# Hybrid decoder trunk: nine of the eleven down-projection chunks of each FFN as seven block products

## The chip, the cores and the metric

The kernel runs on one core of one Trainium2 chip. The metric is the device time of one execution in microseconds (us): the median over the runs shown, beside one execution that the hardware profiler recorded.

## The reference, cut to what matters

Four layers, each a macaron pair: FFN, token mixer, FFN. There are 256 tokens, the model width is 1024 and the FFN width is 2816, all in float32. Eight of the twelve sublayers are this FFN, wrapped in two norms:

```python
def swiglu(x, wg, wu, wd):
    return (jax.nn.silu(x @ wg) * (x @ wu)) @ wd

x = x + 0.5 * rmsnorm(swiglu(rmsnorm(x, g[0]), ffn1_wg[i], ffn1_wu[i], ffn1_wd[i]), g[1])
xn = rmsnorm(x, g[2])          # then the token mixer (convolution, attention or mLSTM)
...
x = x + 0.5 * rmsnorm(swiglu(rmsnorm(x, g[4]), ffn2_wg[i], ffn2_wu[i], ffn2_wd[i]), g[5])
```

## The kernel before, in words

**Precision.** Each float32 operand is split into a high part rounded to the matmul type and a low part, the rest. A product is three matmuls into one accumulator: high by high, high by low, low by high (`products`, L504 to L508).

**Weights.** All weights come from DRAM as one stream of pieces of 128 x 2048 floats (1 MB). SyncE's queue loads piece p into one of `RAW` = 3 raw slots as soon as the split of piece p-3 is complete (`piece_split`). ScalarE makes the high part with `high(p)` (L1103) and VectorE the low part with `low(p)` (L1494), in one of `RING` = 6 slots, which TensorE frees with `piece_used`. The counts of these semaphores are positions in the stream, so the pieces are split in stream order.

**One FFN.** The hidden width of 2816 is worked on as 22 blocks of 128 columns (`BLOCKS`), two to a chunk (11 `CHUNKS`). `block(i)` makes gate and up of one block, 16 products of 256 columns into one PSUM bank, 0 or 1 by turns. ScalarE does `silu_of` (L1147) on the gate half, VectorE `times_up` (L1552) multiplies by the up half and gives h; `h_high` and `h_low` split h into `oT_hi` and `oT_lo`. `down_both(c)` then adds the chunk's part of the output for both tiles of 128 tokens and both halves of 512 columns into banks 4 to 7: eight products, seven of 512 columns and one in two parts of 256. The first four blocks (`early_block`) put the tokens on the partitions, so their h has to be turned over by TensorE (`transpose_h`, L632) before `oT_hi` and `oT_lo` are made.

**Order on TensorE in an FFN.** Early blocks 0 to 3, block 4, `down_both(0)`, block 5, `down_both(1)`, then a loop of units (`unit(c)`: blocks 2c+2 and 2c+3, then `down_both(c)`), then blocks 18 to 21 in a row, and the last stretch: for each tile and half the three chunks 8, 9 and 10. A tile's half is complete, and `y_ready` is signalled, after 18 of these matmuls. `transpose_next`, which turns over tile 0 of the next sublayer's normed input (L547), stands in front of chunk 10 of the last tile and half.

**Order on ScalarE and VectorE.** Both run a fixed list of instructions in order. At the end of an FFN both split two pieces of the next sublayer (`high`/`low` of `w0 + FFN_PIECES + 1` and `+ 2`) after the last split of h, and then come to `joint_part`: squares and their sums on ScalarE (`square_y`, L1112, and `square_x`, L1121), `gain_y` (L1502, L1506, L1509), `update_x` (L1519) and `pre_norm` (L1524, L1529) on VectorE, with small powers on GpSimd between them. They lead from `y_ready` to `xn`, which `transpose_next` reads.

Of the kernel before, what the change touches and what calls it, by code (L numbers as in the profile page):

```python
# [28 lines left out]
P = 128  # L29
D = 1024  # L30
# [10 lines left out]
EARLY = 4  # L41
WARM_UP = 17
# [69 lines left out]

def early_piece(c):

    return 2 * c


def block_piece(i):

    return {4: 4, 5: 6}.get(i, i + i // 2 - 1) if i < BLOCKS - 2 else 3 * CHUNKS - 5 + i - (BLOCKS - 2)  # L120


def down_piece(c):

    return {0: 5, CHUNKS - 3: 3 * CHUNKS - 3, CHUNKS - 2: 3 * CHUNKS - 2, CHUNKS - 1: 3 * CHUNKS - 1}.get(c, 3 * c + 4)


def build(nc, x_in, gains, first_gain, stream, gate_w, gate_b, conv_k, ident_in, rope_in, att_mask_in, ml_mask_in,
          tri_in, out):
    with ExitStack() as ctx:  # L130
# [52 lines left out]

        region = sb("region", [P, REGION])
        used = [0]
# [31 lines left out]
        h = from_region([2, SEQ])  # L217
# [33 lines left out]
        hT_split = sem("hT_split")  # L251
        oT_high_done = sem("oT_high_done")
# [132 lines left out]

        H_SPLITS = EARLY // 2 + BLOCKS - EARLY

        def splits_up_to(i):
            return EARLY // 2 + i - EARLY + 1

        def h_slot(i):

            return i % 4 if i < BLOCKS - 2 else 4 + i - (BLOCKS - 2)
# [105 lines left out]
        def _(pe):  # L499
# [4 lines left out]
            def products(acc, lh, ll, rh, rl, start, stop):  # L504

                nc.tensor.matmul(acc, lh, rh, start=start, stop=False)  # L506
                nc.tensor.matmul(acc, lh, rl, start=False, stop=False)  # L507
                return nc.tensor.matmul(acc, ll, rh, start=False, stop=stop)  # L508
# [50 lines left out]
            def ffn(sub):  # L559
                h0, s0, w0 = BLOCKS * ffn_no(sub), H_SPLITS * ffn_no(sub), w_of(sub)  # L560

                def bank_free(i):
                    if i >= 2:

                        pe.wait_ge(h_ready, h0 + i - 1)
# [24 lines left out]
                def block(i, p, turn=0, before=0):  # L590

                    bank_free(i + before)
                    weights_ready(p + RING * turn)
                    for e in range(2):
                        for k in range(KD):
                            cols = slice(k * 256 + e * P, k * 256 + (e + 1) * P)
                            last = products(ps[:, GU_BANK + i % 2, e * SEQ:(e + 1) * SEQ], w_high[:, p % RING, cols],
                                            w_low[:, p % RING, cols], xT_high()[:, k, :], xT_low()[:, k, :],
                                            k == 0, k == KD - 1)
# [37 lines left out]
                def down(c, p, t, turn=0):  # L637

                    weights_ready(p + RING * turn)
                    for half in range(2):  # L640
                        for j in range(FT):
                            cols = slice(j * D + half * 512, j * D + half * 512 + 512)
                            tok, at = slice(t * P, (t + 1) * P), h_slot(FT * c + j)
                            if t == 1 and half == 1 and j == FT - 1:

                                for part in range(2):
                                    some = slice(cols.start + part * 256, cols.start + part * 256 + 256)
                                    last = products(ps[:, Y_BANK + 2 * t + half, part * 256:part * 256 + 256],
                                                    oT_hi[:, at, tok], oT_lo[:, at, tok], w_high[:, p % RING, some],
                                                    w_low[:, p % RING, some], False, False)  # L650
                                continue
                            last = products(ps[:, Y_BANK + 2 * t + half, :], oT_hi[:, at, tok], oT_lo[:, at, tok],
                                            w_high[:, p % RING, cols], w_low[:, p % RING, cols],
                                            c == 0 and j == 0, False)
                    if t == 1:
                        last.then_inc(piece_used, 1)

                def down_both(c, turn=0):

                    if c < EARLY // 2:  # L660
                        pe.wait_ge(hT_split, s0 + c + 1)
                    else:
                        pe.wait_ge(hT_split, s0 + splits_up_to(FT * c + 1) + 4 * turn)
                    for t in range(TILES):
                        down(c, w0 + down_piece(c), t, turn)
# [21 lines left out]
                down_both(0)  # L687
                block(5, w0 + block_piece(5))
                down_both(1)
                with pe.Fori(0, (CHUNKS - 5) // 2) as turn:  # L690
                    unit(2, turn)
                    unit(3, turn)

                for i in range(BLOCKS - 4, BLOCKS):
                    block(i, w0 + block_piece(i))
                for t in range(TILES):
                    for half in range(2):
                        for c in range(CHUNKS - 3, CHUNKS):
                            p = w0 + down_piece(c)
                            if t == 0 and half == 0:  # L700
                                pe.wait_ge(hT_split, s0 + splits_up_to(FT * c + 1))
# [3 lines left out]
                            for j in range(FT):  # L705
# [4 lines left out]
                                                c == CHUNKS - 1 and j == FT - 1)  # L710
# [1350 lines left out]
```

## Time and profile before

| what | value |
|---|---|
| median of 3 runs | 2031.4 us (2030.3 to 2031.6) |
| span of the profiled execution | 2029.3 us |
| TensorE busy, share of the span | 2020.3 us, 100% |
| weight loads (PEld) | 1883.4 us, 93% |
| VectorE (DVE) | 1202.4 us, 59% |
| ScalarE (ACT) | 965.8 us, 48% |
| GpSimd (POOL) | 26.5 us, 1% |

The profiled execution has no time of its own beside its span; the span leaves out what lies before the first and after the last instruction. Matmuls overlap in the records, so their durations exceed the time that one adds: that time is the distance between the starts of two successive ones. A VectorE or ScalarE instruction that does not depend on the one before it also starts some 0.08 us before that one's record ends.

### The profile page before, as it was taken

The numbers are of one execution on the slowest core, as the hardware profiler recorded it, in microseconds if no ns is written. First come the engines' busy times: TensorE is split into PE (matmuls) and PEld (weight loads), VectorE is DVE, ScalarE is ACT, GpSimd is POOL, SyncE is SP. The second block draws the span as 40 slices with busy tenths as digits, with TensorE's granted clock in tenths as the row PEclk, the third lists the DMA queues.
The fourth block names the chain that finished last, engine by engine and source line by source line (L and its number), as shares of the span: only waits on it lengthen the run. The fifth ranks groups of instructions, "written<-read, shape, count | busy, mean of one in ns | idle before, by whom it ended". The sixth has DMA issues, their size and how long they took to land.

```text
span 2029.3 us, 36261 instructions
## 1 busy us (share of the span) xinstructions
PE 2020.3 (100%) x15078; PEld 1883.4 (93%) x15078; DVE 1202.4 (59%) x1335; ACT 965.8 (48%) x1176; POOL 26.5 (1%) x52
## 2 busy tenths in 40 slices
PE   9999999999999999999999999999999999999998
PEld 7999989998999999988998999998999999998998
DVE  6446675556545887766456555656456554676453
ACT  6444544444444665665444444645444444545442
POOL 0000000000000000000000000000000000000000
PEclk9999999999999999999999999999999999999999
DMA  8554646455554644436544655634544655555541
GB/s 319 203 193 158 249 153 242 186 187 208 187 191 161 224 171 164 150 126 249 187 186 172 223 187 188 226 138 177 204 186 166 228 189 196 192 196 194 205 186 63
DMA packets 56270, 386.08 MB, mean 190 GB/s; under 512 B 6752, under 2 KB 7136, under 8 KB 11232
## 3 DMA queue, kind: packets, MB, share of 16 engines
q1 hardware_dynamic: 52416, 372.07, 49.7%
q10 hardware_dynamic: 3744, 12.39, 1.9%
q8 instruction: 88, 1.44, 0.3%
q14 instruction: 22, 0.18, 0.0%
HBM read 383.39 MB, written 1.05 MB: 189 GB/s over the span
## 4 chain that ended last, share of the span: by engine, by line
PE 98%; DVE 1%; issue 0%; DMA 0%; ACT 0%; POOL 0%; DVEq 0%; POOLq 0%
PE ps L506 24%; PE ps L508 24%; PE ps L507 24%; PE ps L512 6%; PE ps L514 6%; PE ps L513 6%; PE ps L525 2%; PE ps L528 2%; PE ps L531 2%; PE ps L547 1%; PE ps L863 0%; PE ps L632 0%; PE ps L839 0%; DVE w_low L1494 0%; PE ps L874 0%
## 5 line engine op out<-in xcount | busy, mean ns | idle before, releaser
L1494 DVE TENSOR_TENSOR w_low<-raw,w_high 128x2048 fp32r<-128x2048 f32 x351 | 801.8, 2290 | 312.9 <-ACT w_high L1103 312.8
L1103 ACT ACTIVATE w_high<-raw 128x2048 fp32r<-128x2048 f32 x351 | 668.8, 1911 | 50.9 <-DMA raw<-stream 41.3
L506 PE MATMUL ps<-xT_both,w_high 128*128 128x256 f32 x2304 | 638.0, 277 | 0.0
L507 PE MATMUL ps<-xT_both,w_high 128*128 128x256 f32 x2304 | 637.0, 276 | 0.0
L508 PE MATMUL ps<-xT_both,w_low 128*128 128x256 f32 x2304 | 636.8, 276 | 0.0
L507 PEld LDWEIGHTS ps<-xT_both,w_high 128*128 128x128 f32 x2304 | 433.2, 188 | 0.0
L506 PEld LDWEIGHTS ps<-xT_both,w_high 128*128 128x128 f32 x2304 | 432.7, 188 | 0.0
L508 PEld LDWEIGHTS ps<-xT_both,w_low 128*128 128x128 f32 x2304 | 432.5, 188 | 0.0
L1147 ACT ACTIVATE region<-ps 128x256 f32<-128x256 f32 x176 | 67.4, 383 | 663.0 <-PE ps L508 641.8
L506 PE MATMUL ps<-w_high,oT_hi 128*128 128x512 f32 (+1 forms) x896 | 337.6, 377 | 0.0
L508 PE MATMUL ps<-w_high,oT_lo 128*128 128x512 f32 (+1 forms) x896 | 335.6, 375 | 0.0
L507 PE MATMUL ps<-w_low,oT_hi 128*128 128x512 f32 (+1 forms) x896 | 335.6, 375 | 0.0
L1552 DVE TENSOR_TENSOR region<-region,ps 128x256 f32<-128x256 f32 x176 | 74.0, 421 | 343.1 <-ACT region L1147 342.9
L512 PE MATMUL ps<-xT_both,w_high 128*128 128x256 f32 x736 | 207.3, 282 | 0.0
L514 PE MATMUL ps<-xT_both,w_high 128*128 128x256 f32 x736 | 204.7, 278 | 0.0
L513 PE MATMUL ps<-xT_both,w_low 128*128 128x256 f32 x736 | 204.7, 278 | 0.0
L508 PEld LDWEIGHTS ps<-w_high,oT_lo 128*128 128x128 f32 x896 | 168.4, 188 | 30.6
L506 PEld LDWEIGHTS ps<-w_high,oT_hi 128*128 128x128 f32 x896 | 168.5, 188 | 30.1 <-issue 0.3
L507 PEld LDWEIGHTS ps<-w_low,oT_hi 128*128 128x128 f32 x896 | 168.6, 188 | 29.3
L512 PEld LDWEIGHTS ps<-xT_both,w_high 128*128 128x128 f32 x736 | 138.7, 188 | 0.7
L513 PEld LDWEIGHTS ps<-xT_both,w_low 128*128 128x128 f32 x736 | 138.5, 188 | 0.0
L514 PEld LDWEIGHTS ps<-xT_both,w_high 128*128 128x128 f32 x736 | 138.3, 188 | 0.0
(180 smaller groups left out, 1827.3 us busy)
## 6 DMA issues: line engine op xcount, KB each, us to landing
raw<-stream SPq DMA_DIRECT2D x351, 1024.0 KB, 4.8
gain<-gains ACTq DMA_DIRECT2D x23, 512.0 KB, 5.0
x<-x_in SPq DMA_DIRECT2D x2, 512.0 KB, 4.5
raw<-stream SPq DMA_DIRECT2D x2, 512.0 KB, 6.3
region<-rope_in SPq DMA_DIRECT2D x1, 512.0 KB, 6.1
out<-x SPq DMA_DIRECT2D x1, 512.0 KB, 2.6
att_mask<-att_mask_in SPq DMA_DIRECT2D x1, 320.0 KB, 6.2
out<-x SPq DMA_DIRECT2D x1, 256.0 KB, 2.1
```

The source lines that it names most:

```text
L506: nc.tensor.matmul(acc, lh, rh, start=start, stop=False)
L507: nc.tensor.matmul(acc, lh, rl, start=False, stop=False)
L508: return nc.tensor.matmul(acc, ll, rh, start=False, stop=stop)
L512: nc.tensor.matmul(acc, lh, rh, start=start, stop=False)
L513: nc.tensor.matmul(acc, ll, rh, start=False, stop=False)
L514: return nc.tensor.matmul(acc, lh, rl, start=False, stop=stop)
L525: nc.tensor.matmul(acc, xT_high()[:, k, tok], w_high[:, slot, cols], start=k == 0, stop=False)
L528: nc.tensor.matmul(acc, xT_low()[:, k, tok], w_high[:, slot, cols], start=False, stop=False)
L1103: nc.scalar.activation(w_high[:, p % RING, :], raw[:, p % RAW, :], ACT.Copy).then_inc(piece_high, 1)
L1147: nc.scalar.activation(silu[:, i % 2, :], ps[:, GU_BANK + i % 2, 0:SEQ], ACT.Silu).then_inc(silu_done, 1)
L1494: nc.vector.tensor_tensor(w_low[:, p % RING, :], raw[:, p % RAW, :], w_high[:, p % RING, :], ALU.subtract).then_inc(piece_split, 1)
L1552: nc.vector.tensor_tensor(h[:, i % 2, :], silu[:, i % 2, :], ps[:, GU_BANK + i % 2, SEQ:2 * SEQ], ALU.mult).then_inc(h_ready, 1)
```

## The change

Nine of the eleven chunks (`SEVENS`) are added with Strassen's scheme in its seven-product form. A chunk's product is a 256 x 256 by 256 x 1024 matmul: two tiles of tokens by two blocks of hidden rows, and two blocks of hidden rows by two halves of 512 columns. Instead of eight products it makes seven, each from one sum of token blocks and one sum of weight blocks, each accumulated in a PSUM bank of its own (1 to 7) over the nine chunks. So:

- The gate and up blocks 4 to 19 all use bank 0, and each waits for `times_up` of the block before it.
- For each such chunk VectorE makes four sums of the weight blocks (`sum_w`, three instructions, written to `sums`, which is the memory of `xn`) and four sums of h (`sum_h`, three instructions). ScalarE and VectorE split three weight blocks as they are (`corners_high`, `corners_low`: 1536 columns) and the four sums (`sums_high`, `sums_low`: 2048 columns, in the place of the piece's `high` and `low`), and seven blocks of h at once (`seven_h_high`, `seven_h_low`: 896 columns).
- `unit(c)` on TensorE is block 2c+2, three of the seven products, block 2c+3, the other four. Unit 8 is added after the loop. VectorE and ScalarE are one or two pieces less ahead of TensorE in the stream than before.
- After chunk 8, ScalarE copies bank 1 out (`first_part_out`) and VectorE joins the seven sums into banks 4 to 7 (`join`, seven instructions of 512 columns). Blocks 20 and 21 run meanwhile. The last stretch has two chunks, 9 and 10, in place of three.

```diff
+SEVEN = ((1, 1, "corner", 0), (6, 3, "corner", 2), (7, 7, "corner", 1), (4, 2, "sum", 3), (5, 5, "sum", 0),
+         (2, 6, "sum", 2), (3, 4, "sum", 1))
+SEVEN_SPLIT = 3
+def gu_bank(i):
+    return GU_BANK + (i % 2 if i < EARLY or i >= BLOCKS - 2 else 0)
...
-                def bank_free(i):
-                    if i >= 2:
+                def bank_free(i, turn=0):
+                    if i == BLOCKS - 1:
+                        pe.wait_ge(first_copied, ffn_no(sub) + 1)
+                    elif EARLY < i <= BLOCKS - 2:
+                        pe.wait_ge(h_ready, h0 + i + 4 * turn)
+                    elif i >= 2:
...
+                def seven(c, first, last, turn=0):
+                    p = w0 + down_piece(c)
+                    if first == 0:
+                        pe.wait_ge(hT_split, s0 + c + 1 + 2 * turn)
+                        weights_ready(p + RING * turn)
+                    for bank, row, kind, col in SEVEN[first:last]:
...
+                        done = products(ps[:, bank, :], oT_hi_flat[:, tok], oT_lo_flat[:, tok], rh, rl, c == 0,
+                                        c == SEVENS - 1)
...
                 def unit(c, turn=0):
-                    block(2 * c + 2, w0 + block_piece(2 * c + 2), turn, 4 * turn)
-                    block(2 * c + 3, w0 + block_piece(2 * c + 3), turn, 4 * turn)
-                    down_both(c, turn)
+                    block(2 * c + 2, w0 + block_piece(2 * c + 2), turn)
+                    seven(c, 0, SEVEN_SPLIT, turn)
+                    block(2 * c + 3, w0 + block_piece(2 * c + 3), turn)
+                    seven(c, SEVEN_SPLIT, len(SEVEN), turn)
...
-                        for c in range(CHUNKS - 3, CHUNKS):
+                        for c in range(CHUNKS - 2, CHUNKS):
                             p = w0 + down_piece(c)
                             if t == 0 and half == 0:
+                                if c == SEVENS:
+                                    pe.wait_ge(joined, 7 * (ffn_no(sub) + 1))
```

VectorE's list for one FFN afterwards (ScalarE's goes with it: `silu_of`, `high`, `corners_high`, `sums_high`, `seven_h_high`):

```python
def unit(c, turn=0):
    p = w0 + block_piece(2 * c + 2)
    times_up(sub, 2 * c + 2, turn)
    low(p + 3, turn)
    low(p + 4, turn)
    sum_w(sub, c + 1, turn)
    times_up(sub, 2 * c + 3, turn)
    sum_h(sub, c + 1, turn)
    corners_low(sub, c + 1, turn)
    seven_h_low(sub, c + 1, turn)
    sums_low(sub, c + 1, turn)
# start: times_up(1) low(4) sum_w(0) corners_low(0) sums_low(0) times_up(2) low(6) times_up(3) sum_h(0) sum_w(1)
#        seven_h_low(0) times_up(4) corners_low(1) sums_low(1) sum_h(1) low(8) seven_h_low(1) low(9) times_up(5)
#        sum_h(2) sum_w(2) seven_h_low(2) corners_low(2) sums_low(2), then units 2 to 7
# end:   times_up(18) low(29) low(30) times_up(19) chunk_low(9) low(31) join times_up(20) low(32) h_low(20)
#        low(33) times_up(21) h_low(21) low(34) low(35)
```

ScalarE's unit: `silu_of(2c+2)`, `high(p+4)`, `corners_high(c+1)`, `silu_of(2c+3)`, `sums_high(c+1)`, `seven_h_high(c+1)`, `high(p+6)`. Its start has `copy_hT` (the turned h from PSUM to SBUF) after `silu_of(3)` and after `silu_of(4)`.

## Rows read from the trace of the kernel before

**Rows 1.** The page, busy time and share of each engine, and the core's clock.

```profile
PE 2020.3 (100%) x15078; PEld 1883.4 (93%) x15078; DVE 1202.4 (59%) x1335; ACT 965.8 (48%) x1176; POOL 26.5 (1%) x52
...
core 0: 2029.3 us, clock 0.999
```

**Rows 2.** Waits of TensorE: us in total, times, longest.

```profile
PE ps L502 <- DVE ones L1487: 1.1, 1, 1.1
```

**Rows 3.** Timeline of TensorE, one `down_both` in the loop: start us, us, instruction.

```profile
68.06 0.28 PE L508 MATMUL ps<-xT_both,w_low 128*128 128x256 f32 x1
68.18 0.39 PE L506 MATMUL ps<-w_high,oT_hi 128*128 128x512 f32 x1
...
72.95 0.28 PE L506 MATMUL ps<-w_high,oT_hi 128*128 128x256 f32 x1
...
73.67 0.29 PE L506 MATMUL ps<-xT_both,w_high 128*128 128x256 f32 x1
```

**Rows 4.** Groups by shape on VectorE: count, busy us, mean ns, idle before.

```profile
L1494 DVE TENSOR_TENSOR w_low<-raw,w_high 128x2048 fp32r<-128x2048 f32 x351 | 801.8, 2290 | 312.9 <-ACT w_high L1103 312.8
L1552 DVE TENSOR_TENSOR region<-region,ps 128x256 f32<-128x256 f32 x176 | 74.0, 421 | 343.1 <-ACT region L1147 342.9
...
L1584 DVE TENSOR_TENSOR region<-region 128x512 f32<-128x512 f32 x24 | 16.6, 692 | 0.8
...
L1558 DVE TENSOR_TENSOR oT_lo<-ps,oT_hi 128x512 fp32r<-128x512 f32 x16 | 11.0, 688 | 0.5
...
L1612 DVE TENSOR_TENSOR w_low<-raw,w_high 128x1024 fp32r<-128x1024 f32 x1 | 1.2, 1219 | 0.0
L1881 DVE CUSTOM_DVE_ANT_0 region<-ps,region 128x128 f32<-128x128 f32 x4 | 1.2, 292 | 16.2 <-PE ps L997 16.2
```

**Rows 5.** Groups by shape on ScalarE.

```profile
L1103 ACT ACTIVATE w_high<-raw 128x2048 fp32r<-128x2048 f32 x351 | 668.8, 1911 | 50.9 <-DMA raw<-stream 41.3 <-PE ps L508 6.3 <-PE ps L514 2.6
...
L1295 ACT ACTIVATE oT_hi<-region 128x512 fp32r<-128x512 f32 x8 | 5.1, 633 | 26.2 <-DVE region L1733 26.2
```

**Rows 6.** Timeline in the loop: `silu_of` after each of two blocks, then `times_up`.

```profile
62.94 0.38 ACT L1147 ACTIVATE region<-ps 128x256 f32<-128x256 f32 x1 [6.65 <-PE ps L508]
...
68.38 0.38 ACT L1147 ACTIVATE region<-ps 128x256 f32<-128x256 f32 x1 [2.95 <-PE ps L508]
...
68.88 0.42 DVE L1552 TENSOR_TENSOR region<-region,ps 128x256 f32<-128x256 f32 x1 [1.09 <-ACT region L1147]
```

**Rows 7.** Timeline of VectorE in the mLSTM: an instruction that waits for the one before.

```profile
1341.80 0.17 DVE L1886 TENSOR_SCALAR region<-region 128x2 f32<-128x2 f32 x1
1342.00 0.16 DVE L1888 TENSOR_TENSOR region<-region 128x2 f32<-128x2 f32 x1
```

**Rows 8.** DMA issues: count, KB each, us from issue to landing.

```profile
raw<-stream SPq DMA_DIRECT2D x351, 1024.0 KB, 4.8
```

**Rows 9.** Timeline at the start of the fourth sublayer, an FFN.

```profile
480.46 0.38 ACT L1147 ACTIVATE region<-ps 128x256 f32<-128x256 f32 x1 [1.42 <-PE ps L508]
...
482.68 4.49 DVE L1494 TENSOR_TENSOR w_low<-raw,w_high 128x2048 fp32r<-128x2048 f32 x2 [1.38 <-ACT w_high L1103]
...
491.71 0.38 PE L632 MATMUL ps<-ident,region 128*128 128x128 f32 x2
...
497.59 0.38 PE L632 MATMUL ps<-ident,region 128*128 128x128 f32 x2
```

**Rows 10.** Timeline at the end of the third sublayer, an FFN.

```profile
454.47 4.49 DVE L1494 TENSOR_TENSOR w_low<-raw,w_high 128x2048 fp32r<-128x2048 f32 x2 [1.38 <-ACT w_high L1103]
458.88 0.15 DVE L1502 TENSOR_SCALAR mean_first<-mean_y 128x1 f32<-128x1 f32 x1
...
459.52 0.60 ACT L1112 ACTIVATE xn<-ps 128x512 f32<-128x512 f32 x1 [2.71 <-PE ps L508]
...
460.24 0.16 DVE L1506 TENSOR_TENSOR mean_eps<-mean_y,mean_first 128x1 f32<-128x1 f32 x1 [0.61 <-ACT xn L1112]
...
464.45 1.28 DVE L1529 SCALAR_TENSOR_TENSOR xn<-x,rstd_x,gain 128x1024 f32<-128x1024 f32 x1 [0.66 <-POOL rstd_x L1954]
...
466.12 1.03 PE L547 MATMUL ps<-ident,xn 128*128 128x128 f32 x8
```

More of the change, by code:

```diff
@@ L588, in early_block, with block @@
                         last.then_inc(gu_ready, 1)
[L590 to L592 removed]
+                def block(i, p, turn=0):
+                    bank_free(i, turn)
                     weights_ready(p + RING * turn)
@@ L635, in transpose_h @@
                         last.then_inc(hT_in_psum, 1)
[L637 to L656, printed above, removed]
@@ L1650, in ffn @@
                 times_up(sub, 1)
                 low(w0 + 4)
-                low(w0 + 5)
+                sum_w(sub, 0)
+                corners_low(sub, 0)
+                sums_low(sub, 0)
                 times_up(sub, 2)
                 low(w0 + 6)
-                low(w0 + 7)
                 times_up(sub, 3)
-                early_h_low(sub, 0)
+                sum_h(sub, 0)
+                sum_w(sub, 1)
+                seven_h_low(sub, 0)
+                times_up(sub, 4)
+                corners_low(sub, 1)
@@ L1658, in ffn @@
+                sums_low(sub, 1)
+                sum_h(sub, 1)
                 low(w0 + 8)
-                times_up(sub, 4)
-                early_h_low(sub, 1)
+                seven_h_low(sub, 1)
                 low(w0 + 9)
-                h_low(sub, 4)
-                low(w0 + 10)
                 times_up(sub, 5)
-                low(w0 + 11)
-                h_low(sub, 5)
-                low(w0 + 12)
-                with dve.Fori(0, (CHUNKS - 5) // 2) as turn:
+                sum_h(sub, 2)
@@ L1669, in ffn @@
+                sum_w(sub, 2)
+                seven_h_low(sub, 2)
+                corners_low(sub, 2)
+                sums_low(sub, 2)
+                with dve.Fori(0, (SEVENS - 3) // 2) as turn:
                     unit(2, turn)
                     unit(3, turn)
-                for i in range(BLOCKS - 4, BLOCKS):
-                    times_up(sub, i)
-                    if i < BLOCKS - 1:
-                        low(w0 + block_piece(i) + 5)
-                    h_low(sub, i)
+                times_up(sub, BLOCKS - 4)
@@ L1676, in ffn @@
+                low(w0 + 29)
+                low(w0 + 30)
+                times_up(sub, BLOCKS - 3)
+                chunk_low(sub, SEVENS)
+                low(w0 + 31)
+                join(sub)
+                times_up(sub, BLOCKS - 2)
+                low(w0 + 32)
+                h_low(sub, BLOCKS - 2)
+                low(w0 + FFN_PIECES)
+                times_up(sub, BLOCKS - 1)
+                h_low(sub, BLOCKS - 1)
                 low(w0 + FFN_PIECES + 1)
```

251 lines of the change are left out of this document (181 added, 70 removed).

## The prediction

> **What bounds the kernel now.** I read the page first: TensorE is busy for the whole span at its full clock, while VectorE works 59% of it and ScalarE 48% [rows 1]. Then the waits of TensorE: after the start-up it waits for nobody that the list names [rows 2]. So the time is the sum of the matmuls' pitches. An edit gains by issuing fewer matmuls, and loses wherever TensorE has to wait. Both have to be counted, since nothing of today's time is a wait that could be won back. The timelines then give the pitches and the cover of each chain.
>
> **What is removed.** The first 21 matmuls of a `down_both`, seven products of 512 columns, take 72.95 - 68.18 = 4.77 us, 0.2272 us each; the whole, with its eighth product in two parts, takes 73.67 - 68.18 = 5.49 us [rows 3]. `seven` issues just such 21 matmuls, so a chunk saves 0.72 us. Chunk 8 stood in the last stretch without the split product (24 x 0.2272 = 5.45) and saves 0.68. That is 8 x 0.72 + 0.68 = 6.4 us an FFN, and **51 us** for eight.
>
> The Trainium skill ("TensorE: Matmul & The Clock Gate", Back-to-back issue gap) gives some 131 ns a matmul of 512 columns in a stream with weight loads. The trace disagrees with 227 ns [rows 3]; by the page the saving would be 72 x 3 x 0.131 = 28 us and everything below would end some 23 us higher. I go by the row.
>
> **What is added, in durations.** VectorE's two-input instructions fit 0.155 us + one column per 1.04 ns: 128 columns 0.29, 256 0.42, 512 0.69, 1024 1.22, 2048 2.29, with PSUM or without [rows 4]. Between them: 896 columns 1.09, 1536 columns 1.76. Two that don't depend on each other overlap by 0.08; a dependent one starts 0.03 after the end of the other (1341.80 + 0.17 to 1342.00) [rows 7]. So `sum_w` = 1.22 + 0.69 + 0.69 + two gaps = 2.66, `sum_h` = 0.29 + 0.42 + 0.29 + gaps = 1.06. ScalarE: 2048 in 1.91 and 512 in 0.63, so 0.832 ns a column [rows 5]: 1536 in 1.49, 896 in 0.95, 1024 in 1.06.
> VectorE per unit is then 0.42 + 2 x 2.21 + 2.66 + 0.42 + 1.06 + 1.68 + 1.01 + 2.21 less overlaps = 13.7 us. The unit on TensorE is two blocks of 68.38 - 62.94 = 5.44 [rows 6] and one `seven` of 4.77, 15.65 us. VectorE fits in, at 88%.
>
> **The loop.** Let P be the end of block 2c+2. `silu_of` starts at P + 0.21 and `times_up` at P + 0.7, ending at 1.13 [rows 6]. The next block needs it now (one bank), after three products of 2.04: 0.85 spare. VectorE does `low`, `low`, `sum_w` until 8.1. Its raw piece is asked for when `sums_low(c)` ends, at P - 1.1, and lands 4.8 later [rows 8], at 3.8; VectorE wants it at 5.5. Block 2c+3 ends at 7.48, `times_up` runs 8.2 to 8.6, `sum_h` to 9.6, `corners_low` to 11.3, `seven_h_low` to 12.3 (ScalarE's `sums_high` and `seven_h_high` are through by 11.0) and `sums_low`, for which the next `seven` waits, ends at 14.6. TensorE comes to it at 15.65. So the loop costs **nothing**, with 1.0 us to spare. Bounds: nothing, and, if the new shapes take 10% more (1.4 us), 0.4 a unit, 48 units, 19 us.
>
> **The start of each FFN.** Times of the fourth sublayer. `silu_of(1)` at 480.46, `low(4)` starts at 482.68 [rows 9] and ends at 484.97. Then `sum_w(0)` to 487.6, `sums_high(0)` on ScalarE to 489.5 (VectorE's `corners_low` lies beside it), `sums_low(0)` to 491.8, `times_up(2)` to 492.2. But TensorE comes to the turning of that h at 491.71 [rows 9]: it waits 0.5. Block 4 (to the next turning 5.9 [rows 9]) ends at 498.15. Meanwhile VectorE does `low(6)`, `times_up(3)` to 494.7, `sum_h(0)` to 495.8, `sum_w(1)` to 498.4 and only then `seven_h_low(0)` to 499.5: `seven(0)` waits 1.35. The list then runs on without a hole: `sums_low(1)` 505.1, `sum_h(1)`, `low(8)`, `seven_h_low(1)` 509.4, `low(9)`, `times_up(5)` 511.9, `sum_h(2)`, `sum_w(2)`, `seven_h_low(2)`, `corners_low(2)`, `sums_low(2)` 520.6; TensorE comes to `seven(2)` at 519.95 and waits 0.65. Together 2.5 us a start, **20 us** for eight. Before, none of this waited. Bounds: 1.3 to 3.7, a `sum_w` less or half one more on each chain.
>
> **The end of each FFN, first wait.** Zero is now the end of block 18; 19 ends at 7.48, `seven(8)` at 10.2, block 20 at 15.65, block 21 at 21.1. VectorE: `times_up(19)` to 8.6, `chunk_low(9)` 9.75 to 11.0 (after ScalarE's 1.06), `low(31)` 11.6 to 13.8, behind `high(31)`; `join`, seven of 0.69 that overlap by 0.08, to 18.1; `times_up(20)`, `low(32)`, `h_low(20)`, `low(33)` to 23.2, `times_up(21)` to 23.5, `h_high(21)`, `h_low(21)` to H = 24.45. TensorE takes block 21, then chunk 9's six matmuls (1.36), and wants that h at 22.45. It waits 2.05. Before, there were two chunks of cover and no `join` in front. Bounds 1.5 to 3 by how a `join` instruction that writes PSUM is priced (0.61 to 0.75); no row has one on VectorE.
>
> **The end, second wait.** This is the large one. After H, `low(34)` and `low(35)` come first, as before: H was 454.47 - 1.38 = 453.09, and they ended at 458.96, H + 5.87 [rows 10]. From `mean_eps` of tile 0 to the end of its `xn` is 464.45 + 1.28 - 460.24 = 5.49 [rows 10]. Before, `mean_eps` waited for the second half of tile 0, squared from 459.52 [rows 10], and `xn` was ready 0.4 before TensorE came to the turning at 466.12. Between that half and the turning lay 18 + 12 matmuls, 6.8 us. With two chunks it is 12 + 6, 4.1 us. That half is now ready at H + 4.15, VectorE frees itself from the two splits at H + 5.8, does the first `gain_y`, `mean_eps` at H + 6.5, `xn` at H + 12.0. TensorE has 36 matmuls from H on (0.06 + 8.18) and comes at H + 8.24: it waits 3.75. All of this stands before the turning and nothing gives it back, since the next sublayer starts behind it. Seven FFNs have a next sublayer: 7 x (2.05 + 3.75) = 41; the last one has no pieces 33 to 35 to split, and waits 0.4. **41 us.** Bound below: were the two splits not in the way, `mean_eps` would come at H + 5.1 and the wait be 2.4.
>
> **The sum.** -51 + 0 + 20 + 41 = +10 us on the profiled 2029.3, which lies 2 us under the median of 2031.4: **2041 us**. Own range, from the bounds: 2031 to 2052.
>
> **The rivals.**
> (a) The other side: the turning isn't late, because tile 0's norm is ready when TensorE comes. Then the ends cost 14 us and not 41, and the time is 2015. For it speaks that today this chain never holds TensorE up [rows 2]; against it, that it is 5.49 + 0.8 us long and its cover falls from 6.8 to 4.1. It decides once the waits of an FFN together are under 6.4 us rather than 7.8: 1.4 less is enough for break-even, just what the two splits add. 0.15.
> (b) The waits are a little shorter everywhere (1.2 us an FFN): no change, 2031. 0.12.
> (c) VectorE becomes the bound of the loop. It needs 2.0 us more per unit in all, or 1.0 in the half behind `times_up(2c+3)`. For it: 88% load and three engines in a ring. Against: shapes near these are steady in the rows. At 10% more, 2060. 0.10.
> (d) The clock. It was granted in full, 0.999 of it [rows 1], while TensorE never stood still. Waits of some 4 us next to another of 2 are new. If after each long wait the next early block (5.5 us) ran at the lower level of 1.2 GHz and so took twice as long, that is 7 x 5.5 = 38 us, 2079; half of it is as likely, 2060. No row here shows a matmul at the lower level. The Trainium skill ("TensorE: Matmul & The Clock Gate", Part 1) says an idle stretch that is long enough lets the clock fall to half until the engine has been busy again; no row can bear it out. 0.06.
> My forecast holds 0.57.
>
> **How the numbers follow.** 0.2% is 4 us, about what a measurement of this kernel can tell from no change. Of my forecast's share 0.5 lies above 2035.5 and the rest within the band. Slower: 0.50 + 0.10 + 0.06 = 0.66. Same: 0.07 + 0.12 = 0.19. Faster: 0.15. The range 2020 to 2060 leaves out most of (a) and the upper part of (c) and (d).
>
> **What would show it.** TensorE's waits should be some 60 us: behind `times_up(2)` 0.5, `seven_h_low(0)` 1.35, `sums_low(2)` 0.65, `h_low(21)` 2.05 and `xn` 3.75 per FFN, none in the loop. VectorE's busy time should rise by 72 x 5.6 + 56 x 0.69 = 440 to about 1640 us (80%). If the wait in front of the turning is under 2.4, the last part is wrong; if waits stand in the loop, (c) is right; if the clock's row falls below 0.98, (d).

## The result: slower, and by more than predicted

| kernel | median us | range, runs | ratio to before, 95% |
|---|---|---|---|
| before | 2031.5 | 2030.3 to 2031.7, 4 | |
| after | 2069.9 | 2068.2 to 2070.9, 4 | 1.019 [1.0177, 1.0203] |

The change costs 38 us (1.9%). The forecast was 2041 with a range to 2060: the direction is right, the size is not.

**The page and the core's clock** of the changed kernel, which answer to [rows 1]:

```profile
PE 2018.0 (98%) x14670; PEld 1871.8 (90%) x14670; DVE 1617.4 (78%) x1831; ACT 1105.6 (53%) x1208; POOL 26.6 (1%) x52
...
core 0: 2069.0 us, clock 0.991
```

The 408 matmuls that went are the intended ones (216 of 512 columns, three for each of 72 chunks, and 192 by not halving a product). Yet TensorE's busy time fell by only 2.3 us, and the clock is no longer full. VectorE rose to 78%, near the 80% expected.

**The waits of TensorE** in the changed kernel (us in total, times, longest), where [rows 2] had one row:

```profile
PE ps L592 <- DVE xn L1619: 24.4, 7, 3.5
PE ps L551 <- DVE oT_lo L1662: 6.9, 8, 1.0
PE ps L551 <- DVE oT_lo L1715: 6.4, 8, 0.8
PE ps L683 <- DVE region L1642: 4.3, 9, 1.5
```

They are the turning, `seven_h_low(0)`, `h_low(21)` and `times_up(2)`: all four foreseen at these places, 42 us together where 60 were expected, and none in the loop. So 51 us saved and 42 us of waits would have made 2022. About 47 us came from elsewhere, and none of them is in this list.

**Where the time of one FFN went.** The fourth sublayer, cut at the same instructions of TensorE's timeline in three kernels (us; the third is the last experiment below):

| stretch | before | after | difference | predicted | eight chunks, split |
|---|---|---|---|---|---|
| turning of tile 0 to block 4 | 25.73 | 28.88 | +3.15 | +0.5 | 26.28 |
| block 4 to the first product of chunk 0 | 5.88 | 6.92 | +1.04 | +1.35 | 6.92 |
| chunk 0, block 5, chunk 1 | 16.55 | 15.31 | -1.24 | -1.44 | 15.34 |
| blocks 6 to 17 with chunks 2 to 7 | 98.32 | 96.40 | -1.92 | -3.67 | 94.91 |
| block 18 to the next turning | 36.76 | 41.67 | +4.91 | +5.12 | 37.58 |
| sum | 183.24 | 189.18 | +5.94 | +1.86 | 181.03 |

Two stretches show something new: the first, and the loop, where no wait stands. The last one agrees with the forecast in part by luck: blocks 18 to 21 take 0.8 us more than before (22.61 and 21.78), and the waits behind them are shorter by about as much.

**The loop.** TensorE's timeline of the changed kernel, start and duration, at both ends of two blocks of 48 matmuls:

```profile
362.14 0.39 PE L553 MATMUL ps<-corner,oT_lo 128*128 128x512 f32 x1
362.37 0.28 PE L551 MATMUL ps<-xT_both,w_high 128*128 128x256 f32 x1
362.49 0.28 PE L552 MATMUL ps<-xT_both,w_high 128*128 128x256 f32 x1
...
368.02 0.39 PE L551 MATMUL ps<-w_high,oT_hi 128*128 128x512 f32 x1
...
370.51 0.39 PE L553 MATMUL ps<-w_high,oT_lo 128*128 128x512 f32 x1
370.74 0.28 PE L551 MATMUL ps<-xT_both,w_high 128*128 128x256 f32 x1
...
376.39 0.39 PE L551 MATMUL ps<-corner,oT_hi 128*128 128x512 f32 x1
```

A block takes 368.02 - 362.37 = 5.65 us, and so does the next; [rows 6] gave 5.44, and the timeline of before has 5.44 to 5.46. That is 0.1177 us a matmul in place of 0.1134, at an unchanged record duration of 0.28: only the distance between starts shows it. The products of 512 columns run at (370.74 - 368.02) / 12 = 0.2267, as forecast. Before a block there now stands a product of 512 columns; before the change it was the halved product, 256 columns wide [rows 3].

**The end, and the clock.** The same timeline at the turning. The last field is the idle time before it and what ended it:

```profile
472.81 0.39 PE L553 MATMUL ps<-w_high,oT_lo 128*128 128x512 f32 x1
476.68 1.11 PE L592 MATMUL ps<-ident,xn 128*128 128x128 f32 x4 [3.48 <-DVE xn L1619]
...
478.30 0.78 PE L551 MATMUL ps<-w_high,oT_hi 128*128 128x512 f32 x1
478.87 0.63 PE L552 MATMUL ps<-w_low,oT_hi 128*128 128x512 f32 x1
479.30 0.63 PE L553 MATMUL ps<-w_high,oT_lo 128*128 128x512 f32 x1
```

And the windows over it: length, busy time of PE, PEld, DVE, ACT and POOL, granted clock, DMA share, GB/s:

```profile
470.00:475.00 5.00, 3.20 (x15) 2.30 (x13) 3.33 (x7) 1.66 (x4) 0.79 (x2) 1.00 0.93 388
475.00:480.00 5.00, 3.32 (x12) 3.03 (x13) 3.32 (x5) 1.26 (x3) 0.30 (x1) 0.53 0.02 7
480.00:485.00 5.00, 5.00 (x19) 3.98 (x19) 2.91 (x5) 3.32 (x4) 0.55 (x1) 0.79 0.00 0
485.00:490.00 5.00, 5.00 (x23) 4.11 (x22) 3.03 (x4) 0.72 (x3) 0.55 (x1) 1.00 0.44 159
```

After the wait of 3.5 us TensorE runs at its lower level of 1.2 GHz: matmuls of 512 columns stand 0.43 apart, not 0.227. The granted clock is 0.53, then 0.79, then full. Matmuls at the lower level follow all seven turnings behind an FFN, for a shorter or a longer time; in the kernel before they follow none. Rival (d) took place, and here it costs 5.77 - 3.17 = 2.6 us (from the turning to the fifth matmul of the next block, 482.45, against the same distance before). From tile 0's turning to tile 1's the seven places take 1.4 to 2.9 us longer than before, 15.0 us together.

**The chain of VectorE** that makes the turning late, its timeline in the changed kernel, which answers to [rows 10]:

```profile
464.26 0.43 DVE L1715 TENSOR_TENSOR oT_lo<-region,oT_hi 128x256 fp32r<-128x256 f32 x1 [0.48 <-ACT oT_hi L1240]
466.06 4.49 DVE L1584 TENSOR_TENSOR w_low<-raw,w_high 128x2048 fp32r<-128x2048 f32 x2 [1.38 <-ACT w_high L1148]
...
471.13 0.15 DVE L1596 TENSOR_TENSOR mean_eps<-mean_y,mean_first 128x1 f32<-128x1 f32 x1
...
475.34 1.28 DVE L1619 SCALAR_TENSOR_TENSOR xn<-x,rstd_x,gain 128x1024 f32<-128x1024 f32 x1 [0.66 <-POOL rstd_x L2122]
```

`h_low(21)` ends at H = 464.69, the two splits at H + 5.86 (predicted 5.8), `mean_eps` starts at H + 6.4 (6.5) and `xn` ends at H + 11.9 (12.0). The chain was read right to 0.1 us.

**New shapes of VectorE**, its groups by shape: count, busy us and mean ns, idle time before:

```profile
L1682 DVE TENSOR_TENSOR corner<-raw,corner 128x1536 fp32r<-128x1536 f32 x72 | 126.1, 1752 | 0.0
L1671 DVE TENSOR_TENSOR xn<-raw 128x1024 f32<-128x1024 f32 x72 | 87.9, 1220 | 0.0
L1662 DVE TENSOR_TENSOR oT_lo<-region,oT_hi 128x896 fp32r<-128x896 f32 x72 | 78.1, 1085 | 0.0
```

Predicted: 1.76, 1.22 and 1.09 us.

### The profile page after: what moved, and what is told of

Same layout as the page of the kernel before. It is cut to its first block, busy times and chain, and to the rows that moved or that the text cites. A ratio compares the mean times of both kernels' runs of the same rounds, so it can differ in the third digit from the quotient of the medians.

```text
span 2069.0 us, 36195 instructions
## 1 busy us (share of the span) xinstructions
PE 2018.0 (98%) x14670; PEld 1871.8 (90%) x14670; DVE 1617.4 (78%) x1831; ACT 1105.6 (53%) x1208; POOL 26.6 (1%) x52
## 4 chain that ended last, share of the span: by engine, by line
PE 81%; DVE 13%; ACT 3%; issue 1%; DMA 0%; POOL 0%; DVEq 0%; POOLq 0%; ACTq 0%
PE ps L551 19%; PE ps L553 19%; PE ps L552 19%; PE ps L557 6%; PE ps L559 6%; PE ps L558 6%; DVE w_low L1584 6%; ACT w_high L1148 2%; PE ps L592 1%; PE ps L570 1%; PE ps L573 1%; PE ps L576 1%; DVE w_low L1689 1%; DVE xn L1671 1%; ACT w_high L1223 1%
## 5 line engine op out<-in xcount | busy, mean ns | idle before, releaser
L1584 DVE TENSOR_TENSOR w_low<-raw,w_high 128x2048 fp32r<-128x2048 f32 x279 | 632.3, 2288 | 113.2 <-ACT w_high L1148 113.2
L551 PE MATMUL ps<-xT_both,w_high 128*128 128x256 f32 x2304 | 647.9, 281 | 0.0
L553 PE MATMUL ps<-xT_both,w_low 128*128 128x256 f32 x2304 | 647.2, 281 | 0.0
L552 PE MATMUL ps<-xT_both,w_high 128*128 128x256 f32 x2304 | 647.2, 281 | 0.0
L1148 ACT ACTIVATE w_high<-raw 128x2048 fp32r<-128x2048 f32 x279 | 531.9, 1911 | 28.5 <-DMA raw<-stream 17.3
L551 PE MATMUL ps<-w_high,oT_hi 128*128 128x512 f32 x544 | 217.7, 400 | 6.4 <-DVE oT_lo L1715 6.4
L552 PE MATMUL ps<-w_low,oT_hi 128*128 128x512 f32 x544 | 214.9, 395 | 0.0
L553 PE MATMUL ps<-w_high,oT_lo 128*128 128x512 f32 x544 | 214.8, 395 | 0.0
L557 PE MATMUL ps<-xT_both,w_high 128*128 128x256 f32 x736 | 207.7, 282 | 0.0
L558 PE MATMUL ps<-xT_both,w_low 128*128 128x256 f32 x736 | 205.2, 279 | 0.0
L559 PE MATMUL ps<-xT_both,w_high 128*128 128x256 f32 x736 | 205.2, 279 | 0.0
L1223 ACT ACTIVATE w_high<-xn 128x2048 fp32r<-128x2048 f32 x72 | 138.0, 1917 | 54.0 <-DVE xn L1676 54.0
L1689 DVE TENSOR_TENSOR w_low<-xn,w_high 128x2048 fp32r<-128x2048 f32 x72 | 164.7, 2287 | 2.5 <-ACT w_high L1223 2.5
L1216 ACT ACTIVATE corner<-raw 128x1536 fp32r<-128x1536 f32 x72 | 107.2, 1489 | 73.2 <-DMA raw<-stream 73.1
```

Of the source, the lines that this page charges most:

```text
L551: nc.tensor.matmul(acc, lh, rh, start=start, stop=False, skip_group_check=goes_on)
L552: nc.tensor.matmul(acc, lh, rl, start=False, stop=False, skip_group_check=goes_on)
L553: return nc.tensor.matmul(acc, ll, rh, start=False, stop=stop, skip_group_check=goes_on)
L558: nc.tensor.matmul(acc, ll, rh, start=False, stop=False)
L559: return nc.tensor.matmul(acc, lh, rl, start=False, stop=stop)
L1148: nc.scalar.activation(w_high[:, p % RING, :], raw[:, p % RAW, :], ACT.Copy).then_inc(piece_high, 1)
```

## The experiments

What was to be told apart: how much the blocks' pitch costs and what sets it; what the clock costs; and whether the waits at the two ends of an FFN can be had back by reordering, or only by more cover.

| kernel | median us | ratio to before, 95% | span, clock |
|---|---|---|---|
| `b_nosplit` | 2056.5 | 1.0124 [1.0107, 1.0141] | 2054.5, 0.999 |
| `a_split` | 2053.7 | 1.0111 [1.0094, 1.0128] | 2051.8, 0.993 |
| `a_splitfirst` | 2074.7 | 1.0198 [1.0179, 1.0217] | 2074.0, 0.992 |
| `a_warm` | 2056.6 | 1.0124 [1.0107, 1.0141] | 2053.1, 0.999 |
| `a_lows` | 2062.7 | 1.0152 [1.0135, 1.0169] | 2061.8, 0.995 |
| `a_low33` | 2071.3 | 1.0197 [1.0182, 1.0213] | 2069.4, 0.992 |
| `a_start` | 2082.4 | 1.0252 [1.0237, 1.0268] | 2079.7, 0.995 |
| `a_all` | 2062.7 | 1.0152 [1.0138, 1.0166] | 2060.9, 0.999 |
| `a_best1` | 2041.6 | 1.0049 [1.0035, 1.0062] | 2038.5, 1.000 |
| `a_best2` | 2042.3 | 1.0051 [1.0037, 1.0064] | 2040.8, 0.999 |
| `eight_plain` | 2026.0 | 0.9972 [0.9962, 0.9983] | 2024.1, 1.000 |
| `eight_split` | 2013.6 | 0.9914 [0.99, 0.9927] | 2011.8, 1.000 |

### The pitch alone: the kernel before without its halved product (`b_nosplit`)

```diff
-                            if t == 1 and half == 1 and j == FT - 1:
+                            if False:
```

> The kernel before (2031 us), with the split product as one of 512 columns and nothing else changed. Theory 1: the first block behind each down_both (and the blocks that follow without a break, if the pitch holds on) goes from 0.1134 to 0.1177 us a matmul: 9 to 17 blocks x 0.2 us x 8 = 15 to 28 us slower, less 8 x 8 x 0.05 = 3 for the split's own cost, 2043 to 2056 us. Rival: 2028 us, as only the split's own cost goes.

Measured: 25 us slower, with three matmuls fewer a chunk, the clock in full and no new wait of any size. Its timeline shows 96 matmuls, two blocks:

```profile
520.64 0.39 PE L508 MATMUL ps<-w_high,oT_lo 128*128 128x512 f32 x1
520.86 0.28 PE L506 MATMUL ps<-xT_both,w_high 128*128 128x256 f32 x1
...
532.17 0.39 PE L506 MATMUL ps<-w_high,oT_hi 128*128 128x512 f32 x1
```

(532.17 - 520.86) / 96 = 0.1178. The sum closes: 17 blocks x 48 x 0.0043 x 8 = 28 us, less some 3 us since 24 matmuls of 0.2267 take 5.44 and not 5.49. So the halved product of the kernel before is worth 25 us, and the change drops it.

### The halved product put back (`a_split`), at the other end of the group (`a_splitfirst`)

```diff
+                        if 0 < c < SEVENS - 1 and bank == SEVEN[last - 1][0]:
+                            for part in range(2):
+                                some = slice(part * 256, part * 256 + 256)
+                                done = products(ps[:, bank, some], oT_hi_flat[:, tok], oT_lo_flat[:, tok], rh[:, some],
+                                                rl[:, some], False, c == SEVENS - 1)
+                            continue
```

`a_splitfirst` has `SEVEN[first][0]` in the condition: the product behind the block is halved, not the one ahead of it. Chunks 0 and 8 are left as they are in both.

> The changed kernel (2070 us), with the last product before each block in two parts of 256 columns, as in the kernel before, for chunks 1 to 7. Chunk 8 keeps whole products and is the control inside the run. Theory 1, a block of 256-column matmuls runs at 0.1177 us a matmul when matmuls of 512 columns stand right before it, and at 0.1134 when some of 256 do: blocks 6 to 18 go to 0.1134, block 20 stays at 0.1177; 14 blocks x 0.2 us x 8 FFNs = 22 us less for TensorE, of which the waits at the FFNs' ends take back some 5, so 2050 to 2056 us. Rival, the slower pitch comes from the one bank, the memory layout or the busier VectorE and ScalarE: nothing changes, 2070 us.

> As a_split (2054 us), but the product in two parts is the first one of each part of a seven and not the last, so matmuls of 512 columns stand right before each block again. If the slow pitch comes from the neighbour right before the block, blocks run at 0.1177 us a matmul and the time is 2070 us. If it comes from how many matmuls stand between two blocks, or from a 256-column matmul anywhere between them, blocks stay at 0.1137 and the time is 2054 us.

Measured: `a_split` gains 16 us over the changed kernel, `a_splitfirst` nothing (its interval overlaps the changed kernel's) with the very same number of matmuls. Inside `a_split` one timeline holds both cases, block 18 behind the halved product of chunk 7 and block 19 behind a whole one of chunk 8:

```profile
430.09 0.28 PE L553 MATMUL ps<-w_high,oT_lo 128*128 128x256 f32 x1
430.21 0.29 PE L551 MATMUL ps<-xT_both,w_high 128*128 128x256 f32 x1
...
435.67 0.39 PE L551 MATMUL ps<-corner,oT_hi 128*128 128x512 f32 x1
...
437.50 0.39 PE L553 MATMUL ps<-corner,oT_lo 128*128 128x512 f32 x1
437.72 0.28 PE L551 MATMUL ps<-xT_both,w_high 128*128 128x256 f32 x1
...
443.38 0.39 PE L551 MATMUL ps<-w_high,oT_hi 128*128 128x512 f32 x1
```

5.46 us against 5.66. It is the width of what stands right ahead of the block that counts here. Over the whole trace of `a_split` there is no exception among the blocks from 5 on: most of those behind 256 columns run at 0.1134 to 0.1138 (the first of them in an FFN up to 0.1148), all behind 512 columns at 0.1177 to 0.1179. (`a_start` below has exceptions.) A halved product itself costs 0.03 to 0.05 us more. Thirteen blocks of an FFN are fast in this kernel (6 to 18), not the 14 that were expected: 13 x 0.2 x 8 = 21 us, less 13 halved products, 3 to 5 us, leaves the 16 us measured.

### The clock alone (`a_warm`)

Fifteen matmuls of 512 columns, whose results nobody reads, stand before the turning, in the time in which TensorE waited:

```diff
                             if t == 1 and half == 1 and c == CHUNKS - 1:
+                                for _ in range(15 if sub + 1 < SUBLAYERS else 0):
+                                    nc.tensor.matmul(ps[:, 0, :], oT_hi[:, 0, 0:P], w_high[:, p % RING, 0:512],
+                                                     start=True, stop=True)
                                 transpose_next(sub)
```

> The changed kernel, with 15 matmuls of 512 columns (3.4 us) into bank 0, whose result nobody reads, in the wait of 3.5 us in front of the turning of the next sublayer's input, seven times. Theory 2, that wait lets TensorE's clock fall to the lower level for the 5 us behind it and costs 2.7 us each time: the granted clock stays at 1.00, 2070 - 19 = 2051 us. Rival, the clock falls for another reason or the fall is hidden by other waits: 2066 to 2070 us.

Measured: 13.3 us faster than the changed kernel by the medians, 15.9 by the profiled spans, though it does more. The turning comes no earlier: from block 18 to it the fourth sublayer still takes 41.67 us. The gain is all behind it. The windows of this kernel over the turning show the full clock:

```profile
470.00:475.00 5.00, 4.91 (x27) 3.89 (x26) 2.69 (x5) 2.56 (x6) 0.55 (x1) 1.00 0.32 128
475.00:480.00 5.00, 5.00 (x24) 4.09 (x23) 4.23 (x6) 3.65 (x5) 0.55 (x1) 1.00 0.00 0
```

So the fall of the clock is worth 13 to 16 us, some 2 us a turning; the 15.0 us that the changed kernel loses between tile 0's turning and tile 1's are gone here (each of the seven is within 0.2 us of the kernel before). The Trainium skill ("TensorE: Matmul & The Clock Gate", Part 1) says that an idle stretch that is long enough halves the clock until the engine has been busy again. The traces agree, with 0.53 granted behind 3.5 us of waiting and 1.00 once the wait was filled.

### The end by reordering (`a_lows`, `a_low33`)

`a_lows` takes `low(34)` and `low(35)` out of the way, behind the first tile's `xn` and its `xT`. `a_low33` moves `low(33)` behind `h_low(21)`:

```diff
                 h_low(sub, BLOCKS - 1)
-                low(w0 + FFN_PIECES + 1)
-                low(w0 + FFN_PIECES + 2)
```

```diff
-                low(w0 + FFN_PIECES)
                 times_up(sub, BLOCKS - 1)
                 h_low(sub, BLOCKS - 1)
+                low(w0 + FFN_PIECES)
```

> The changed kernel, with VectorE's splits of the next sublayer's pieces 1 and 2 moved from the end of the FFN to behind xn of tile 0 and behind xT of tile 0. Theory 3, those two splits put xn of tile 0 off by 1.4 us: the wait in front of the turning falls from 3.5 to 2.1 us, and the clock doesn't fall any more if that is short enough: 2070 - 10 = 2060 us, and 2041 us with the clock. Rival, the next sublayer's first blocks then wait for the moved splits instead: 2066 us or more, with waits of TensorE for w_low.

> The changed kernel (2070 us), with the split of piece 33 (the next sublayer's first) behind h_low(21) in VectorE's list and not in front of times_up(21). VectorE now stands idle 0.5 and 1.4 us around h_low(21), behind ScalarE. If its list is what sets xn of tile 0, piece 33's split fills the second of these holes: the wait for h_low(21), 0.8 us, goes, and xn comes 1.4 us earlier, so 7 x 1.4 = 10 us less and a little more by the clock, 2057 to 2060 us. Rival, the list isn't what binds there: only the waits trade places, 2068 us.

Measured: `a_lows` is 7 us faster than the changed kernel, `a_low33` is not (+1.4). Waits of TensorE, first `a_lows`:

```profile
PE ps L592 <- DVE xn L1619: 19.6, 11, 2.2
```

then `a_low33`:

```profile
PE ps L592 <- DVE xn L1619: 29.3, 7, 4.2
PE ps L551 <- DVE oT_lo L1715: 3.8, 8, 0.5
```

In `a_lows` the first turning waits 2.23 us in place of 3.48, near the 2.4 that the prediction gave for this case; but four turnings of tile 1 now wait as well, and after a wait of 2.23 the clock still falls at most places: matmuls 0.42 to 0.43 us apart follow five of the seven turnings, for shorter times (0.995 granted over the whole kernel, 0.991 in the changed one). In `a_low33` what `h_low(21)` gains (6.4 to 3.8) the turning loses (24.4 to 29.3). VectorE has no room for the splits: ahead of the turning they put off tile 0's norm, behind it tile 1's.

### The start by reordering (`a_start`)

```diff
-                sum_w(sub, 1)
                 seven_h_low(sub, 0)
+                sum_w(sub, 1)
```

> The changed kernel, with seven_h_low(0) ahead of sum_w(1) in VectorE's list. If the wait of TensorE in front of the first seven comes from that place in the list, it falls from 0.85 us to nothing in each FFN, 8 x 0.85 = 7 us, 2063 us. Rival, VectorE's list has no hole there and all that follows comes later by the 1 us that seven_h_low then waits for ScalarE: the wait moves to the second or third seven, 2068 to 2072 us.

Measured: 12.5 us slower. Rows that have grown or are new among TensorE's waits, of `a_start`:

```profile
PE ps L551 <- DVE oT_lo L1662: 13.1, 9, 1.6
...
PE ps L551 <- ACT region L1197: 5.0, 8, 0.9
PE ps L551 <- DVE w_low L1689: 3.1, 8, 0.4
```

ScalarE's list was left as it was: `sums_high(1)` waits for the later `sum_w(1)`, and `silu_of(4)` and `copy_hT(1)`, which TensorE needs, are queued behind it. In the fourth sublayer the wait in front of the first seven is gone as intended, and 0.67 us inside it and 1.6 us in front of the second have come. Moving an instruction on one engine moves all that stands behind its consumer on another.

This trace also shows that the rule of the pitch is not complete. Block 5 stands behind a product of 512 columns here too, and in the fourth sublayer it runs at (523.16 - 517.82) / 47 = 0.1136:

```profile
517.01 0.50 PE L551 MATMUL ps<-w_high,oT_hi 128*128 128x512 f32 x1 [0.67 <-ACT region L1197]
...
517.82 0.28 PE L551 MATMUL ps<-xT_both,w_high 128*128 128x256 f32 x1
...
523.16 0.28 PE L553 MATMUL ps<-xT_both,w_low 128*128 128x256 f32 x1
```

Five of the eight blocks 5 and two of the blocks 7 of `a_start`, and one block 5 of `a_all`, are fast like this. TensorE had waited inside the products ahead of each of them, but it had ahead of slow blocks of this kernel too. From the last matmul of 512 columns to the block's first it is 0.233 to 0.236 us ahead of the fast ones and 0.226 to 0.229 ahead of the slow ones. So a product of 512 columns ahead is not enough by itself for the slow pitch, and what sets it is not known.

### All of it at once (`a_all`, `a_best1`, `a_best2`)

`a_all` joins `a_split`, `a_start`, `a_lows`, the later `low(33)`, a turning one product later and 6 unread matmuls ahead of it. `a_best1` leaves out `a_start` and `a_lows` and takes the halved product, the later `low(33)`, the later turning, and 8 unread matmuls; of these the later `low(33)` had not helped by itself, and the later turning was not measured by itself. `a_best2` adds to it a new order at the start on both engines:

```diff
-                sum_w(sub, 1)
+                corners_low(sub, 1)
                 seven_h_low(sub, 0)
                 times_up(sub, 4)
-                corners_low(sub, 1)
-                sums_low(sub, 1)
+                sum_w(sub, 1)
                 sum_h(sub, 1)
-                low(w0 + 8)
+                sums_low(sub, 1)
                 seven_h_low(sub, 1)
+                low(w0 + 8)
```

(on ScalarE `sums_high(1)` goes behind `copy_hT(1)`, `high(8)` behind `seven_h_high(1)`).

> All mendings together in the changed kernel: split products before blocks, seven_h_low(0) early, the splits of pieces 33 to 35 behind the last h and the norm of tile 0, the turning one product later in the last stretch, six matmuls that keep TensorE busy in what is left of the wait. From 2070: pitch -16, start -5, clock -13, ends 7 x (1.4 + 0.8 + 0.6) = -20, of which some 5 return as waits in the faster stream: about 2021 us, under the kernel before by 0.5%. Rival, the moved splits make the next sublayer wait, as a_lows showed in part: 2035 us.

> a_low33, with the split products of a_split, the turning one product later in the last stretch, and eight matmuls that keep TensorE busy in what is left of the wait. If the causes add up: 2070 - 16 (pitch) - 13 (clock) - 10 (piece 33) - 5 (turning) = 2026 us, or 2030 us with 4 us of waits that come back in the faster stream; level with the kernel before or just under. If they overlap, 2040 us.

> a_best1, with the lists at the FFN's start reordered on both engines: VectorE does corners_low(1) in the time in which ScalarE makes seven_h_high(0), and sum_w(1) after times_up(4); ScalarE does silu_of(4) and copy_hT(1) before it waits for sum_w(1), which held them up in a_start. If what a_start lost was the two instructions queued behind that wait, this gives 0.5 to 1 us an FFN, 4 to 8 us below a_best1. Rival, the whole start is bound by VectorE's work between times_up(1) and sums_low(2), and the order moves the wait to the third seven: the same as a_best1.

Measured: 2062.7, 2041.6 and 2042.3. `a_all` was expected at 2021, or 2035 by the rival, and missed both; it shows that the edits don't add up: its waits spread over seven rows of 3.8 us or more, of which `a_start` brings 4.6 and 4.3 and the later `xT` 7.1. `a_best1` comes out near the 2040 given for overlapping causes and is, with `a_best2`, the best form with nine chunks, still 10 us slower than before. What is left of waits in it:

```profile
PE ps L592 <- DVE xn L1628: 12.1, 7, 1.8
PE ps L551 <- DVE oT_lo L1671: 8.0, 8, 1.7
PE ps L551 <- DVE oT_lo L1724: 3.8, 8, 0.5
```

To 12.1 come the 56 unread matmuls, 56 x 0.227 = 12.7, together as much as the 24.4 of the changed kernel: TensorE stands without useful work in front of the turning for as long as ever, only warm. In `a_best2` the start's 8.0 become 1.2, and a new 7.0 appears behind `w_low` L1698 (`sums_low`), for the third group of products. That is the rival's outcome: the wait moves along with the order, and its sum stays (8.0 and 8.2), so VectorE's work binds the start in both orders.

### More cover: eight chunks (`eight_split`, `eight_plain`)

No list tried shortened the end by more than 7 us, so the cover is given back: `SEVENS` = 8, and chunk 8 is added in the last stretch as in the kernel before. `join` then lies beside blocks 18 to 21, which use banks 0 and 1 by turns:

```diff
-SEVENS = 9
+SEVENS = 8
...
-    return GU_BANK + (i % 2 if i < EARLY or i >= BLOCKS - 2 else 0)
+    return GU_BANK + (i % 2 if i < EARLY or i >= BLOCKS - 4 else 0)
...
-                        for c in range(CHUNKS - 2, CHUNKS):
+                        for c in range(CHUNKS - 3, CHUNKS):
```

and VectorE's end becomes:

```python
unit(SEVENS - 2)
times_up(sub, 16)
low(w0 + 26)
low(w0 + 27)
times_up(sub, 17)
chunk_low(sub, 8)
low(w0 + 28)
join(sub)
times_up(sub, 18)
...
times_up(sub, 19)
chunk_low(sub, 9)
...
times_up(sub, 20)
...
h_low(sub, 20)
...
times_up(sub, 21)
h_low(sub, 21)
```

> Only eight chunks (0 to 7) are made as seven products; chunks 8, 9 and 10 form the last stretch as in the kernel before, blocks 18 to 21 run in a row in banks 0 and 1 by turns, and the product that stands right before each block (chunks 1 to 6) is made in two parts of 256 columns. The computation is complete. If the end's waits came from the short last stretch, and the blocks' pitch from the 512-column product in front of them, both are gone: 8 FFNs save 8 x 0.72 = 5.8 us each (46), the starts still cost about 1.4 us each (11), and the row of blocks 18 to 21, behind a seven that isn't split, is slow (4 x 0.2 x 8 = 6): 1998 to 2006 us, clock 0.999, no wait behind xn. The rival: the end's chain is bound by VectorE's own backlog (the join and the four splits), whatever TensorE has as cover: then waits behind xn stay near 24 us and the clock falls, 2025 to 2035.

> The same with eight chunks, but no product is made in two parts. If the pitch of the blocks hangs on the product before them, all 96-matmul groups behind a 512-column product run at 0.1178 and the kernel is 14 to 20 us slower than its split form, 2014 to 2024 us. If the pitch was a matter of the waits and the clock at the end of an FFN, which are gone here, the two kernels agree within 4 us.

Measured: both beat the kernel before, `eight_split` by 18 us (0.9%), `eight_plain` by 5.5 us (0.3%). The clock of `eight_split` and its waits of TensorE:

```profile
core 0: 2011.8 us, clock 1.000
```

```profile
PE ps L555 <- DVE oT_lo L1680: 7.7, 8, 1.6
PE ps L687 <- DVE region L1660: 2.8, 8, 0.4
...
PE ps L596 <- DVE xn L1635: 0.3, 1, 0.3
```

The turning and `h_low(21)` have gone from the list, and the clock is full: the rival (VectorE's backlog binds whatever the cover) has fallen. (These two kernels also have `join` two blocks earlier in VectorE's list; no run parts this from the longer last stretch.) The two forms differ by 12.4 us where 14 to 20 were expected: the pitch returns in kernels with no wait at the end and no fall of the clock, so it is a cost of its own. I had `eight_split` too low by 8 us, and the table by stretches says where: blocks 5 and 17 run behind whole products of chunks 0 and 7 and are slow too (six slow blocks, 6 x 0.2 x 8 = 10, not four, 6); the eleven halved products of an FFN cost some 0.04 each, 4 us together; and the first unit, which waits a little for VectorE, takes 15.93 and not 15.77. Halving the products of chunks 0 and 7 that stand ahead of a block as well would be the next thing to try. It was not tried.

## Why the prediction was wrong, by its own steps

**What bounds the kernel now.** Right: the time is the sum of pitches, and each wait counts in full. But it took the pitches as fixed.

**What is removed.** Right in itself: `seven` takes 21 x 0.2267 = 4.76 us (4.89 for the first one of an FFN), forecast 4.77. The Trainium skill ("TensorE: Matmul & The Clock Gate", Back-to-back issue gap) gives some 131 ns a matmul of 512 columns in a stream with weight loads. The changed kernel disagrees as the kernel before did, with 227 ns.

**The loop: this is the step that failed.** "The unit on TensorE is two blocks of 68.38 - 62.94 = 5.44": they take 5.65 each. No wait arose and VectorE did fit in, as said. But the unit took 16.07 us and not 15.65, and so saved 0.32 over 16.39 and not 0.72. Over 17 blocks of 8 FFNs it is 28 us (17 x 48 x 0.0043 x 8), against the bounds of 0 to 19 that I had given to other reasons. The prediction read that the kernel before halves one product of eight, counted it only as 0.04 us of cost, and didn't ask what the following matmuls did at it. Nothing in the trace of before would have given the price, since there every loop block stands behind the halved product; but block 4, which stands behind a turning, ran at (497.59 - 491.71 - 0.14) / 48 = 0.1196 [rows 9] (0.14 for the two turnings of h), and this should have warned that a block's pitch depends on its neighbour.

**The starts.** Predicted 2.5 us each. Measured by distances between starts in the fourth sublayer, 1.04 (1.35 predicted) for `seven_h_low(0)` and 0.56 (0.5) for `times_up(2)`; the 0.65 of `sums_low(2)` did not come. In that sublayer `sums_low(2)` ends at 533.28 and its product starts at 533.44. Reckoned from the turning ahead of block 4, VectorE got there 0.5 us earlier than in the sum, and TensorE later, since blocks 5 and 6 take 0.2 us more each. By TensorE's list the starts cost 11 us in place of 20.

**The end, first wait.** 0.8 in place of 2.05 an FFN by the list, 1.1 by distances between starts. In the third sublayer block 18 ends at 440.66; TensorE wants the last h at 463.74, 23.08 later and not 22.45, since blocks 19, 20 and 21 take 0.2 us more each; VectorE has it at 464.69, 24.03 later and not 24.45. So 0.63 us of the miss is the pitch and 0.42 a VectorE that was reckoned too slow. In `a_split`, whose blocks 19 to 21 are slow still, the wait stays the same (6.3 in total).

**The end, second wait.** 7 x 3.5 = 24.4 in place of 26, right. The lower bound of 2.4 without the two splits was right as well: 2.23 in `a_lows`.

**Rival (d), the clock.** It had 0.06 and came about at all seven turnings, beside my forecast and not in its place. Its price was set at 38 us (a whole early block at the lower level) or, as likely, half of that, 19; it is 13 to 16 us, since the clock is back after some 6 us. Its sign was set wrong: the clock's row was to fall below 0.98, and it fell to 0.991 with all seven places in it. The mistake was to count it as another case. The forecast itself had waits of 3.75 us in a kernel whose TensorE had never stood still, so it should have carried this term.

**The sum.** For the profiled spans: -51 (removed) + 42 (waits) + 28 (pitch) + 16 (clock) = +35, and measured is +39.7. The rest lies mostly in how a wait is counted, since the list leaves out what the restart costs beside the idle time. In the fourth sublayer the four waits are 5.4 us by the list and 6.4 by distances between starts (3.64 and 1.14 in the last stretch, 1.04 and 0.56 at the start), and with the latter it closes: -6.5 (removed) + 6.4 + 3.5 (pitch) + 2.6 (clock) = +6.0, measured 5.94. The waits, forecast 18 us too long in all, hid part of what was missing, and that was luck: without it the forecast would have been further off.

## What to carry to other kernels

A product written in an odd way next to a block may be there for its neighbour's pitch: before removing it, compare the distance between starts in blocks with different neighbours, since busy times and waits don't show it. A shorter stretch of matmuls can cost twice when a chain of another engine ends in it, once as a wait and once through the clock. Where that chain was full, neither of the two orders tried won more than 7 us, and more cover took the wait away. Here a smaller dose of the change (eight chunks and not nine) kept the gain and lost both costs.

## What the runs showed of the hardware that was not expected

- In the FFN's blocks from 5 on, matmuls of 256 columns are 0.1134 to 0.1138 us apart behind matmuls of 256 columns, and 0.1177 to 0.1179 behind those of 512, but for seven blocks of `a_start` and one of `a_all`, which are fast behind 512 columns. The difference persists over 96 and 192 matmuls and is set anew at the next group. Why is open. It is not the whole rule: the mixers' first 60 such matmuls, which stand behind the turning and six matmuls of 512 columns, run at 0.1133 to 0.1135 in three sublayers of the kernel before and at 0.1178 in the fourth.
- Half-speed matmuls followed a wait of 3.5 us seven times in seven in the changed kernel, and a wait of 2.23 us five times in seven (`a_lows`). In `a_split` they followed six of seven such waits and not the one before the turning at 1105.23, though it is as long as the others (3.5 us). A wait of 1.7 to 1.8 us behind eight more matmuls was followed by none, in seven of seven (`a_best1`).
